# Index heads in row halves, a half-depth slab for key and steps, rotary halves exchanged by ScalarE, and VectorE's weight remainders ahead of the first selection

## What is computed

```python
h = rms_norm(x, w)
proj = h @ w_in
(q, k, v, qi, ki, wi, z, xbc, dt_raw, g_attn, g_ssd) = jnp.split(proj, offsets, axis=-1)
q  = apply_partial_rope(q, cos_a, sin_a);  k  = apply_partial_rope(k, cos_a, sin_a)
qi = apply_partial_rope(qi, cos_i, sin_i); ki = apply_partial_rope(ki, cos_i, sin_i)
# index scores: 8 heads of 64, one key
rel = jax.nn.relu(jnp.einsum('bqhd,bsd->bqhs', qi, ki))
score = jnp.where(causal, jnp.einsum('bqhs,bqh->bqs', rel, wi), -jnp.inf)
_, sel = lax.top_k(score, 64)            # attention sees the selected keys only
dt = jax.nn.softplus(dt_raw + dt_bias)   # step sizes of the Mamba-2 branch
xbc = jax.nn.silu(causal_dwconv_2(xbc, conv_w, conv_b))
```

## Time and profile before

| | |
|---|---|
| median of three runs | 1697.97 us |
| the profiled execution | 1699.4 us |
| its span (first to last instruction) | 1697.6 us |
| granted clock of TensorE over the span | 0.997 of full speed |
| busy: PE, DVE, ACT, POOL | 1676.8, 1336.8, 1078.0, 704.4 us |

### The profile page before, as it was taken

How to read it: one execution, slowest core, us unless ns; L and a number is a source line. 1 busy time by engine, 2 the same in 40 slices (tenths; PEclk the granted TensorE clock), 3 DMA queues, 4 the chain that set the end, 5 groups by cost and what they waited for, 6 DMA issues and landing times. The chain is left out here.

```text
span 1697.6 us, 28621 instructions
## 1 busy us (share of the span) xinstructions
PE 1676.8 (99%) x11034; PEld 1513.7 (89%) x11034; DVE 1336.8 (79%) x2161; ACT 1078.0 (64%) x1809; POOL 704.4 (41%) x434
## 2 busy tenths in 40 slices
PE   9999999999999999999999999999999999999997
PEld 8998889988888899999778988899999878888887
DVE  7968887494887879975996599778986698669795
ACT  7676576676765573776654676656477765377572
POOL 8631115962210383444554621057344455361113
PEclk9999999999999999999999999999999999999999
DMA  8546655641665654554345456555465345546562
GB/s 309 165 149 192 211 168 180 199 124 53 194 188 188 198 174 151 179 194 125 125 161 187 148 178 215 166 186 187 137 199 167 123 133 170 174 141 199 189 184 87
DMA packets 81240, 288.43 MB, mean 170 GB/s; under 512 B 9168, under 2 KB 9680, under 8 KB 80976
## 3 DMA queue, kind: packets, MB, share of 16 engines
q1 hardware_dynamic: 79776, 283.15, 52.7%
q10 hardware_dynamic: 1328, 3.44, 0.6%
HBM read 285.21 MB, written 1.05 MB: 169 GB/s over the span
## 5 line engine op out<-in xcount | busy, mean ns | idle before, releaser
L1472 ACT ACTIVATE w_hi<-w_raw 128x1024 fp32r<-128x1024 f32 (+1 forms) x544 | 545.0, 1036 | 268.4 <-PE lin L786 176.1
L547 POOL TENSOR_TENSOR w_lo<-w_raw,w_hi 128x1024 fp32r<-128x1024 f32 (+1 forms) x205 | 502.1, 2462 | 354.9 <-ACT w_hi L1472 222.1
L547 DVE TENSOR_TENSOR w_lo<-w_raw,w_hi 128x1024 fp32r<-128x1024 f32 (+1 forms) x339 | 489.7, 1448 | 33.1 <-ACT w_hi L1472 31.3
L784 PE MATMUL lin<-hid_pair,w_hi 128*128 128x256 f32 x1168 | 334.8, 287 | 0.6 <-POOL w_lo L547 0.6
L785 PE MATMUL lin<-hid_pair,w_hi 128*128 128x256 f32 x1168 | 330.7, 283 | 0.0
L786 PE MATMUL lin<-hid_pair,w_lo 128*128 128x256 f32 x1168 | 330.7, 283 | 0.0
L784 PEld LDWEIGHTS lin<-hid_pair,w_hi 128*128 128x128 f32 x1168 | 224.2, 192 | 2.7 <-issue 2.2
L785 PEld LDWEIGHTS lin<-hid_pair,w_hi 128*128 128x128 f32 x1168 | 224.3, 192 | 0.3
L786 PEld LDWEIGHTS lin<-hid_pair,w_lo 128*128 128x128 f32 x1168 | 224.2, 192 | 0.0
L556 POOL TENSOR_TENSOR hid_pair<-arena,hid_pair 128x256 fp32r<-128x256 f32 x64 | 55.1, 867 | 327.5 <-ACT std L1540 179.0
L805 PE MATMUL logit<-h_pair,w_hi 128*128 128x512 f32 x540 | 146.7, 392 | 0.0
(11 more groups left out here) (385 smaller groups left out, 3564.8 us busy)
## 6 DMA issues: line engine op xcount, KB each, us to landing
w_raw<-in_upA SPq DMA_DIRECT2D x112, 512.0 KB, 4.2
w_raw<-in_upB SPq DMA_DIRECT2D x64, 512.0 KB, 4.3
w_raw<-in_xbc SPq DMA_DIRECT2D x48, 512.0 KB, 4.5
w_raw<-in_dnA SPq DMA_DIRECT2D x32, 512.0 KB, 4.3
w_raw<-in_dnB SPq DMA_DIRECT2D x32, 512.0 KB, 3.6
w_raw<-in_z SPq DMA_DIRECT2D x32, 512.0 KB, 4.4
w_raw<-in_gates SPq DMA_DIRECT2D x32, 512.0 KB, 4.2
w_raw<-in_ps SPq DMA_DIRECT2D x32, 512.0 KB, 4.3
```

The costliest lines, as they stand in the source:

```text
L547: eng.tensor_tensor(w_lo[slab.slot][:, half, part], w_raw[slab.slot][:, half, part], w_hi[slab.slot][:, half, part].bitcast(F32), ALU.subt ...
L784: nc.tensor.matmul(out, lhs[0], rhs[0], start=first, stop=False)
L1472: nc.scalar.activation(w_hi[slab.slot][:, half, part], w_raw[slab.slot][:, half, part], ACT.Copy)\
```

## The change

The order of the slabs is now `qi` (2), `kidtwi` (1), `k`, and so on: `kidtwi` is the third. It is a slab of half the depth a half: 128 output features, whose eight input chunks lie four in each half, so that the roundings and remainders of its halves are 512 wide instead of 1024. TensorE multiplies it with `one_half_products`, 24 matmuls in place of 48.

An index head now lies in one row half of its chunk (rows 0 to 63 or 64 to 127), and the key lies once in each row half of one chunk. An index product contracts over 64 rows.

The ropes of the index queries take three VectorE instructions of 128 partitions. Before them ScalarE copies the rotary halves crosswise, in four copies of 32 partitions by 512 elements per slab, into `stat` and `tr`. The key's rope has five instructions on 64 or 32 partitions. The score row of the first 128 tokens is held in PSUM (`tr`) in place of SBUF.

VectorE's programme between the slabs is written in another order. The first index scores come one slab later; the first four rounds of the top eights, the selection and two parts of the step sizes move into the stage `xbc`; the remainders of `xbc` slabs 1 and 2 (half 1) are formed right after the last rope, those of slabs 3 and 4 behind the taps of slabs 0 and 1; the remainder of slab 5 keeps its place ahead of the taps of slab 3. The second tokens' scores and rounds come one slab later.

The diff, cut to its core:

```diff
-SECOND = [("kidtwi", 1), ("qi", 2), ("k", 1), ("q", 4), ("v", 1), ("xbc", 12), ("z", 8),
+SECOND = [("qi", 2), ("kidtwi", 1), ("k", 1), ("q", 4), ("v", 1), ("xbc", 12), ("z", 8),
 def depth(stage, n):
+    if stage == "kidtwi":
+        return KC // 2
...
+            def one_half_products(slab, rhs, waits):
+                wait_hi, wait_lo = waits
+                out = lin[slab.bank][:, 0, :]
+                slab.wait_bank_free(pe)
+                for k in range(KC):
+                    half, at = k // slab.depth, k % slab.depth
+                    if at == 0:
+                        slab.wait_split(pe, half)
+                    w = tile_of(slab, half, at)
+                    wait_hi(k)
+                    nc.tensor.matmul(out, w[0], rhs[k][0], start=(k == 0), stop=False)
+                    nc.tensor.matmul(out, w[1], rhs[k][0], start=False, stop=False)
+                for k in range(KC):
+                    half, at = k // slab.depth, k % slab.depth
+                    wait_lo(k)
+                    mm = nc.tensor.matmul(out, tile_of(slab, half, at)[0], rhs[k][1], start=False, stop=(k == KC - 1))
...
+                        lo = ID * (head % 2)
                         mm = nc.tensor.matmul(logit[:, 2 * (i % 2) + i // 2, 0:(t + 1) * P],
-                                              qi2[:, head // 2, t * P:t * P + P],
-                                              ki2[:, head % 2, 0:(t + 1) * P], start=True, stop=True)
+                                              qi2[lo:lo + ID, head // 2, t * P:t * P + P],
+                                              ki2[lo:lo + ID, 0, 0:(t + 1) * P], start=True, stop=True)
...
+                slab = slab_at("kidtwi", 0, l)
+                slab.wait_done(act)
+                nc.scalar.activation(dscr[0:WI_AT + IH, 2, :], lin[slab.bank][0:WI_AT + IH, 0, :], ACT.Identity,
+                                     bias=pcol2(l, "dt_bias")[0:WI_AT + IH, :]).then_inc(s.rope_in, 1)
+                for r in range(2):
+                    slab_at("qi", r, l).wait_released(act)
+                    for at in range(0, P, ID):
+                        for to, of in ((at, at + half), (at + half, at)):
+                            ins = nc.scalar.activation(qi_swap[r][to:to + half, :, :], first_two[of:of + half, r, :, :], ACT.Copy)
+                    ins.then_inc(s.qi_swapped, 1)
+                weights_hi(slab.ahead(ROUND_AHEAD))
...
+                def rope_index_queries(r, cos, sin):
+                    out = qi2[:, 2 * r:2 * r + 2, :]
+                    dve.wait_ge(s.qi_swapped, 2 * l + r + 1)
+                    tt(out, first_two[:, r, :, :], cos, ALU.mult)
+                    mixer.link(tt(qi_swap[r], qi_swap[r], sin, ALU.mult))
+                    tt(out, out, qi_swap[r], ALU.subtract).then_inc(s.rope_done, 1)
...
-                    row = ix_sc[:, 0, 0:n]
+                    row = tr[:, T:T + n] if t == 0 else ix_sc[:, 0, 0:n]
...
+                for n in range(4):
+                    weights(slab_at("q", n, l))
+                    rope(q2[:, 2 * n:2 * n + 2, :], slab_at("q", n, l), *tables("attn"))
+                    if n in (1, 2):
+                        index_work(n - 1)
+                weights(slab_at("v", 0, l))
+                weights(slab_at("xbc", 0, l))
+                index_work(2)
...
                 def xbc_taps(slab, n, j):
-                    weights(slab)
+                    if n >= 3:
+                        weights(slab)
                     older_taps(...)
+                    if n < 2:
+                        weights(slab_at("xbc", n + 1, l))
                     if n == 0:
                         step_sizes(3)
                     elif n == 1:
-                        index_scores(1, 0)
-                    elif n == 2:
-                        index_scores(1, 1)
-                    elif 3 <= n < 3 + rounds:
-                        top_eights(1, range(n - 3, n - 2))
+                        index_work(3)
+                    elif n < 4:
+                        index_scores(1, n - 2)
+                    else:
+                        top_eights(1, range(n - 4, n - 3))
```

More of the change, by code:

```diff
@@ L726, in _ @@
             for l in range(2):
-                opening("kidtwi", 2 + l, l)
-                weights("qi", l, both=True)
+                opening("qi", 2 + l, l)
+                weights("kidtwi", l, both=True)
                 for stage in ("k", "q", "v"):
@@ L1623, in opening @@
                 scaled(MIXER_OPENING[layer], scaled_set(layer)[0])
-                first.wait_released(act)
-                evict(first, 0)
+                if evict is not None:
+                    first.wait_released(act)
+                    evict(first, 0)
                 done(second)
-                second.wait_released(act)
-                evict(second, 1)
+                if evict is not None:
+                    second.wait_released(act)
+                    evict(second, 1)
             def out_of(slab, n, half):
@@ L2375, in rope @@
[L2375 to L2383, removed]
+                    tt(out, lin[slab.bank][:, :, :], cos, ALU.mult)
@@ new lines, in rope, with rope_index_key @@
+                    dve.wait_ge(s.rope_done, 8 * l + r)
+                    for to, of in ((lower, upper), (upper, lower)):
+                        ins = tt(part[to, :, :], lin[slab.bank][of, :, :], sin[of, :, :], ALU.mult)
+                    ins.then_inc(s.bank_free[slab.bank], 1)
+                    slab.wait_released(dve)
+                    tt(out, out, part, ALU.add).then_inc(s.rope_done, 1)
+                def rope_index_key(slab, cos, sin):
+                    own, copy, half = slice(ID, P), slice(0, ID), ID // 2
+                    raw, part, out = lin[slab.bank][:, 0, :], lin[slab.bank][:, 1, :], ki2[:, 0, :]
+                    rope_unit[0] += 1
+                    slab.wait_done(dve)
+                    tt(out[own, :], raw[own, :], cos[own, 0, :], ALU.mult)
+                    for to, of in ((slice(ID, ID + half), slice(ID + half, P)), (slice(ID + half, P), slice(ID, ID + half))):
+                        ins = tt(part[to, :], raw[of, :], sin[of, 0, :], ALU.mult)
+                    mixer.link(ins)
+                    tt(out[own, :], out[own, :], part[own, :], ALU.add).then_inc(s.bank_free[slab.bank], 1)
+                    slab.wait_released(dve)
+                    nc.vector.tensor_copy(out[copy, :], out[own, :]).then_inc(s.rope_done, 1)
@@ L2441, in selection @@
                     ix.link(tt(sel[:, t, 0:n], sel[:, t, 0:n], const(f"causal{t}", n), ALU.add))
-                for n in range(2):
-                    rope(qi2[:, 2 * n:2 * n + 2, :], slab_at("qi", n, l), *tables("idx"))
+                dve.wait_ge(s.rope_in, l + 1)
+                stt(mag, arg, -1.0, arg, ALU.mult, ALU.max).then_inc(s.dt_abs, 1)
+                rope_index_key(slab_at("kidtwi", 0, l), *tables("idx"))
+                for r in range(2):
+                    rope_index_queries(r, *tables("idx"))
                 take_over(dve, "k", 1, l)
@@ L2448, in layer, with index_work @@
                 rounds = TOPK // 8
-                for n in range(4):
-                    weights(slab_at("q", n, l))
-                    rope(q2[:, 2 * n:2 * n + 2, :], slab_at("q", n, l), *tables("attn"))
+                def index_work(n):
                     if n < 2:
@@ L2509, in xbc_taps @@
                         da_probs(0)
-                assert COUNT["xbc"] >= rounds + 3
+                assert COUNT["xbc"] == rounds + 4
                 slabs("xbc", xbc_taps, l)
@@ L2700, in constants @@
         for at in bases:
[L2701 to L2702 removed]
+            to = at + dim // 2
+            cos[at:at + half] = cos[to:to + half] = np.cos(ang)
+            sin[at:at + half], sin[to:to + half] = np.sin(ang), -np.sin(ang)
         put(f"cos_{name}", cos)
         put(f"sin_{name}", sin)
[L2705 to L2707 removed]
     q, k = np.arange(T)[:, None], np.arange(T)[None, :]
@@ L2758, in index_rows @@
     lower, upper = rotary_rows(ID)
-    chunks = [np.concatenate([first + h * ID + part for part in (lower, upper) for h in (2 * c, 2 * c + 1)])
+    chunks = [np.concatenate([first + h * ID + part for h in (2 * c, 2 * c + 1) for part in (lower, upper)])
               for c in range(n // 2)]
```

80 lines of the change are left out of this document (35 added, 45 removed).

## The result

The changed kernel takes **1703.74 us** (median of 10 runs, 1702.11 to 1706.44), the kernel before 1698.44 us beside it (10 runs): ratio 1.0024, 95% interval 1.0013 to 1.0035. It is slower by about 5 us (0.24%). The forecast was 1703.0.

The account below looks back on a forecast made before the run. TensorE was taken as busiest, with VectorE's chain feeding it deciding what a saving keeps. Slab 6 coming 2.5 us later in each of two layers adds 5.0: 1704.4 profiled, 1703.0 median; range 1701 to 1705, over all cases 1693 to 1707.

Parts of the forecast that it names:

- Stage and limit: Whole kernel: TensorE busy 1676.8 of 1697.6 us; where the change lies, VectorE, feeding it, busy 5.86 of 6 us.
- TensorE's saving: In `kidtwi`: 24 matmuls fewer at 0.12 us, 2.9 us a layer, 5.8 in all; index products counted the same.
- VectorE up to slab 2: Ropes to `xbc` slab 2: VectorE out of the ropes at 634.1 instead of 634.7, slab 2's remainder starting at 667.9.
- The new wait: Step sizes behind slab 3's remainder: line 2068 finds GpSimd in its 2.4 us remainder, a new 2.3 us a layer.
- The idle stretches: VectorE in `xbc`: 1.45 us idle on ScalarE's copy, then 1.5 waiting for the roundings before slab 4's remainder.
- TensorE's stalls: TensorE waits for GpSimd's remainders: 0.2 us at `k`, about 0.4 at slab 4, 3 at 5, 1.7 at 6.
- The sum: Per layer: 5.3 us of waits against 2.9 saved, slab 6 coming 2.5 us later; two layers make 5.0.
- The median: Whole kernel: profiled execution 1699.4 to 1704.4 us, median 1.4 below that, thus 1703.0.
- (a): Behind slab 3's remainder: no wait, 2.3 us a layer fall away, 1698.4 us; chance 0.30.
- (b): `xbc` slabs: VectorE's chain keeps ahead of TensorE, slab 6's half 0 there by 701.5, 1692.6 us; chance 0.13.
- (c): Behind slab 2's start, say at the second tokens' scores: one more such wait, 2.4 us a layer, 1707.8 us; chance 0.13.

Follow-up runs that it names:

- e2: Changed kernel with three VectorE moves: step sizes ahead of slab 3's remainder, second four rounds and first selection ahead of slab 4's, attention mask one slab later; 1693.01 us.
- e4: Kernel before with only the changed kernel's VectorE order (first tokens' score row in PSUM), none of the other edits; 1711.33 us.
- e1: Changed kernel with one move: in xbc slab 0 the step sizes stand ahead of the remainder of slab 3; 1697.38 us.
- e9: Changed kernel, VectorE's order untouched, with GpSimd's half of xbc slab 3 held back until the step sizes are done; 1699.75 us.
- e11: The changed kernel measured again, unaltered, on another chip; 1703.66 us.
- e12: The same kernel as e2 measured again, on the same chip as e11; 1692.02 us.
- e10: Changed kernel with four rounds and selection ahead of slab 4's remainder and the mask one slab later, step sizes still behind slab 3's remainder; 1699.72 us.
- e6: e2 with the attention mask put back behind the scores in xbc slab 3, ahead of slab 6's remainder; 1694.61 us.
- e7: e4 with the step sizes moved ahead of the remainder of slab 3; 1703.71 us.
- e5: e2 with all index products taking queries and keys from the lower 64 rows instead of alternating halves; 1696.61 us.

## Why the prediction was right

- **Stage and limit.** TensorE at 99% with a feeder at 98%: less work for TensorE turned into waits for GpSimd's remainders, 8.5 us in all where there had been 1.1. In e2, where only the 0.2 us at `k` is left of them in the layer, the saving is kept.
- **TensorE's saving.** 24 matmuls at 0.12 us, 2.9. The layer of e2, 3.7 us shorter, bears this out: 2.9, and 1.3 of the index products (2 x 0.18 + 2 x 0.48), less 0.2 for the wait at `k` and 0.3 in the products next to the index groups. I had counted the index products the same. The Trainium skill ("TensorEngine Tiling (Array Packing)", section "Theoretical Speedup") gives up to twofold for a contraction of 64. The runs show 22% and 31% less time, not a half.
- **VectorE up to slab 2.** Forecast: idle 1.6 ahead of line 2497, the ropes done at 634.1, the remainder of slab 2 at 667.9. Measured, in before's clock: 1.45, 634.5, and the second of the pair at 667.7. I had two reasons for this time, and in the changed kernel VectorE's own work sets it: ScalarE's rounding of the slab ends at 666.9, 0.75 us ahead. In e4 it is the rounding. The hit is in part luck, since the waits for GpSimd on the way changed places: the first scores took 2.0 us less and line 2056, the like of 2016, 2.2 less, but line 2054 took 2.25 where its like took 0.41, and a remainder among the `q` slabs 3.11 instead of 1.22.
- **The new wait.** Forecast 2.3 us at line 2068, measured 2.38 against 0.28, in both layers. e1 and e9 show its cause from both sides.
- **The idle stretches.** Forecast 1.45 and 1.5, measured 1.52 and 1.33; GpSimd's half of slab 6 forecast 706.7, measured 706.25.
- **TensorE's stalls.** 0.2 at `k`, 0.4, 3 and 1.7 forecast; 0.23, 0.73, 2.84 and 0.12 measured (0.19 in the second layer). The fourth shrank because TensorE itself was late: 1.5 us at the lower clock took its place.
- **The sum.** 2.5 us a layer forecast, 2.17 and 2.04 measured. The chain sets it: from the layer's start slab 6 begins at 89.86 us, 0.14 after its remainder, against 87.74 before, and the forecast's chain ended 0.45 later than the real one. So two things that the forecast lacked did not spoil it, the 1.3 us of the index products and the lower clock, for TensorE reached slab 6 no later than its remainder either way. In TensorE's own account the layer has 3.9 of waits, 1.5 at the lower clock, 0.7 in slower restarts behind the three stalls (against e2, which has none) and 0.3 next to the index groups, less 2.9 and 1.3: 2.2.
- **The median.** It rises by 5.3 us, of which the two layers hold 4.2. The two profiled executions differ by 3.0, since before's had the stretch near 386 us, 1.25, that the other lacked. On the second chip e11 is 4.2 above the kernel before. So about 1 us of the 5.3 is not in the layers; it may be the scatter of such stretches, which I have not traced. That the forecast's 5.0 fits the median better than it fits the layers is luck.
- **Rivals.** (a) is out: line 2068 waits in both layers. (b), 1692.6, is what e2 and e12 reach once the idle stretches and the wait are covered: its condition was put rightly, and it was not met. (c) is out: the second tokens' scores took 1.53 and 2.04 us, as before (1.52 and 2.08), and behind line 2068 no further wait of this kind came in the `xbc` stage.

What stays open: why the same row half is slower than the full height, and what decides whether the clock falls.

## What to carry to other kernels

When the busiest engine is only a hair ahead of its feeder, follow the feeder's chain to the point where its product is used before counting a saving. Behind a VectorE instruction that sets GpSimd going, place work that did not lengthen beside GpSimd's remainders here (six convolution taps with a PSUM operand took 2.42 us either way, a MAX8 0.29), and ahead of an instruction that waits for ScalarE place whatever is due anyway. Three moved calls turned 5 us lost into 6.3 (e2) and 7.5 (e12) won.

## What the runs showed of the hardware

- Clock. Of eight stalls of 2.74 to 2.86 us in the hybrid layers (changed, e11, e4, e10), six went with 3.4 us at granted clock 0.50, which began between 0.4 us before the stall's end and 1.5 us after it; of eleven of 0.9 to 1.8 us there (e1, e6, e7, e9, e4), none. Elsewhere a stall of 1.4 us at 382 us, in all 14 profiles, went with such a stretch in 10 of them, for 3.4 us in five and 6.8 in five. What it costs depends on what follows. In e10, where no stall follows at a later slab, the layer with the stretch is 1.0 us longer than the other. In e4 it costs nothing: the first layer has the stretch and no stall at slab 6, the second has no stretch and a stall of 1.56 us there, and they take 127.42 and 127.66. TensorE's stall at slab 6 in e4's second layer, then e10's two layers, with and without the stretch:

```profile
1254.85 0.36 PE L784 MATMUL lin<-hid_pair,w_hi 128*128 128x256 f32 x1 [1.56 <-POOL w_lo L547]
```

```profile
1230.00:1233.50 3.50, 3.11 (x15) 3.15 (x16) 3.36 (x7) 2.52 (x3) 0.43 (x2) 0.51 0.57 163
692.00:695.50 3.50, 3.42 (x28) 3.45 (x29) 3.36 (x7) 2.41 (x3) 0.49 (x1) 1.00 0.67 199
```

- Index products: contraction 64 in alternating row halves against the same half, TensorE's groups in the changed kernel and in e5:

```profile
636.26 0.71 PE L1289 MATMUL logit<-arena 64*128 64x128 f32 x8
...
649.43 1.13 PE L1289 MATMUL logit<-arena 64*128 64x256 f32 x8
```

```profile
646.38 1.16 PE L1289 MATMUL logit<-arena 64*128 64x128 f32 x8
...
653.41 1.99 PE L1289 MATMUL logit<-arena 64*128 64x256 f32 x8
```

- ScalarE's exchange copies of 32x512 from PSUM to PSUM take 0.57 us each, four in 2.29; I had taken 4.2 for all eight, measured 4.6.
